# Products that nothing reads in the waits of a chunked scan, and three weight tiles ahead of the fourth in the last stage

## What is computed

```python
def step(state, inp):                      # 8 heads of 64, 1024 positions
    r_t, w_t, k_t, v_t, a_t, b_t = inp
    sa = jnp.einsum('bhvk,bhk->bhv', state, a_t)
    state = state * w_t[:, :, None, :] + sa[..., None] * b_t[:, :, None, :] \
            + v_t[..., None] * k_t[:, :, None, :]
    return state, jnp.einsum('bhvk,bhk->bhv', state, r_t)
...
yn = ((y - mu) * lax.rsqrt(var + GN_EPS)).reshape(B, S, RWKV_WIDTH) * lnx_g + lnx_b
y_a = yn + bonus                           # width 512
br_a = (y_a * jax.nn.silu(z_a)) @ w_pa[l]
br_b = (y_b * jax.nn.silu(z_b)) @ w_pb[l]
merged = jax.nn.sigmoid(g_a) * br_a + jax.nn.sigmoid(g_b) * br_b
x = x + gate[:, None, :] * (merged @ w_o[l])
return rms_norm(x, final_g)
```

## Time and profile before

| | us |
|---|---|
| median of 3 runs | 2534.33 |
| the profiled execution's own time | 2538.74 |
| its span, first to last instruction | 2537.0 |
| TensorE busy | 2445.8 (96%) |
| VectorE / ScalarE / GpSimd busy | 1338.9 / 849.6 / 984.2 |
| mean granted TensorE clock, share of full speed | 0.985 |

### The profile page before, as it was taken

How to read it: one execution, slowest core, us unless ns; L and a number is a source line. 1 busy time by engine, 2 the same in 40 slices (tenths; PEclk the granted TensorE clock), 3 DMA queues, 4 the chain that set the end, 5 groups by cost and what they waited for, 6 DMA issues and landing times. The chain is left out here.

```text
span 2537.0 us, 41052 instructions
## 1 busy us (share of the span) xinstructions
PE 2445.8 (96%) x17413; PEld 1984.2 (78%) x17413; DVE 1338.9 (53%) x2078; ACT 849.6 (33%) x1375; POOL 984.2 (39%) x524
## 2 busy tenths in 40 slices
PE   7998999999999999999999989999999998988998
PEld 6887878888888888888887747787786668887786
DVE  6113543253253221222468289999997764456842
ACT  4214553321111120123453266445333662224231
POOL 3221424443243342344565215466462202221774
PEclk9999999999999999999999999999999998899999
DMA  3112413122222211111323412342343002103423
GB/s 141 49 43 83 134 34 108 50 81 88 78 82 87 75 50 42 50 50 50 103 72 126 133 44 81 104 136 82 106 135 146 26 24 89 37 4 110 149 76 115
DMA packets 82085, 207.68 MB, mean 82 GB/s; under 512 B 8392, under 2 KB 21744, under 8 KB 81904
## 3 DMA queue, kind: packets, MB, share of 16 engines
q1 hardware_dynamic: 74992, 192.48, 23.1%
q10 hardware_dynamic: 6912, 12.59, 1.4%
HBM read 170.81 MB, written 35.27 MB: 81 GB/s over the span
## 5 line engine op out<-in xcount | busy, mean ns | idle before, releaser
L332 PE MATMUL ps<-region_rounded,weights_hi_by_slot 128*128 128x512 f32 x2432 | 962.1, 396 | 19.7 <-DVE region_rounded L640 13.6
L334 PE MATMUL ps<-region_rounded,weights_lo_in_place 128*128 128x512 f32 x2432 | 948.8, 390 | 0.0
L333 PE MATMUL ps<-region_rounded,weights_hi_by_slot 128*128 128x512 f32 x2432 | 948.4, 390 | 0.0
L326 POOL TENSOR_TENSOR weights_lo_in_place<-wbuf,weights_hi_by_slot 128x1024 fp32r<-128x1024 f32 x194 | 483.9, 2497 | 670.0 <-ACT weights_hi_by_slot L322 669.7
L332 PEld LDWEIGHTS ps<-region_rounded,weights_hi_by_slot 128*128 128x128 f32 x2432 | 458.0, 188 | 123.1 <-issue 26.5
L333 PEld LDWEIGHTS ps<-region_rounded,weights_hi_by_slot 128*128 128x128 f32 x2432 | 458.1, 188 | 95.6 <-issue 3.6
L334 PEld LDWEIGHTS ps<-region_rounded,weights_lo_in_place 128*128 128x128 f32 x2432 | 457.6, 188 | 95.9
L322 ACT CAST weights_hi_by_slot<-wbuf 128x1024 fp32r<-128x1024 f32 x194 | 201.8, 1043 | 370.7 <-DMA wbuf<-w_mlp 215.7
L2169 DVE MAX8 gcols<-region 128x8 f32<-128x384 f32 (+5 forms) x192 | 171.6, 894 | 6.6
L2171 DVE MATCH_REPLACE8 region<-gcols,region 128x384 f32<-128x384 f32 (+5 forms) x192 | 168.2, 876 | 0.0
L1459 POOL TENSOR_TENSOR region_rounded<-region,region_rounded 128x512 fp32r<-128x512 f32 x64 | 83.0, 1297 | 215.5 <-DVE region_rounded L1612 215.5
(11 more groups left out here) (368 smaller groups left out, 3459.0 us busy)
## 6 DMA issues: line engine op xcount, KB each, us to landing
wbuf<-w_mlp SPq DMA_DIRECT2D x64, 512.0 KB, 3.6
wbuf<-w_hn SPq DMA_DIRECT2D x37, 512.0 KB, 4.1
wbuf<-w_in SPq DMA_DIRECT2D x25, 512.0 KB, 3.7
region<-xT SPq DMA_DIRECT2D x24, 512.0 KB, 6.4
xtra<-w_ada SPq DMA_DIRECT2D x32, 384.0 KB, 4.2
scratch_hn_out<-tmp ACTq DMA_DIRECT2D x48, 256.0 KB, 3.9
region<-scratch_hn_out SPq DMA_DIRECT2D x24, 512.0 KB, 7.7
wbuf<-w_att SPq DMA_DIRECT2D x20, 512.0 KB, 3.7
```

The costliest lines, as they stand in the source:

```text
L326: self.nc.gpsimd.tensor_tensor(self.m.lo4[:, n % SLOTS, :], self.m.raw4[:, n % SLOTS, :], self.m.hi4[:, n % SLOTS, :].bitcast(F32), ALU.su ...
L332: nc.tensor.matmul(out, m.hi4[:, s, w], m.rounded(hi + k, half(hf)), start=(k == 0), stop=False)
L333: nc.tensor.matmul(out, m.hi4[:, s, w], m.rounded(lo + k, half(hf)), start=False, stop=False)
L334: return nc.tensor.matmul(out, m.lo4[:, s, w], m.rounded(hi + k, half(hf)), start=False, stop=(k == KT - 1))
```

## The change

Two edits, which don't touch each other.

In the second scan `in_use(n)` issues n products of the identity (a 128*128 weight load and 64 columns) into columns 256 to 319 of bank 7, which nothing reads; they wait for no semaphore and set none. Three stand in each level 4 and 5 after the second half's y1 and q1 products and before the wait for the first mask, and three between G and W of each pair. In pair 0 eight stand at each of the four places that hold the state's steps in later pairs. In all 8 x 9 + 32 = 104.

In the last stage the first four groups of branch A (c = 0 and 1, both halves, j = 16 to 19) are issued as tiles 0 to 2 of all four, then tile 3 of all four. The waits for weights and bank stand before tile 0, the count in `st.products` after tile 3. The other groups are as before.

```diff
--- before.py
+++ after.py
@@ -2411,6 +2411,7 @@
 
 
 
+
     S = new_semaphore(nc)
     mats, mats_masked = S("chunk_products"), S("chunk_products_masked")
     turned, tok_copied = S("tok_turned"), S("tok_copied")
@@ -2516,6 +2517,10 @@
 
         @block.tensor
         def _(pe):
+            def in_use(n):
+                for _ in range(n):
+                    nc.tensor.matmul(m.ps[:, 7, 256:320], m.const("ident"), m.const("ident")[:, 0:64], start=True, stop=True)
+
             def chunk_products(i):
                 for par in range(2):
                     if i:
@@ -2597,6 +2602,8 @@
                 if l > 1:
                     before.then_inc(q1, 1)
                 n = 2 * (LAST * i + l - 1)
+                if l > 3:
+                    in_use(3)
                 pe.wait_ge(y1_masked, n + 1)
                 if l == 1:
                     pe.wait_ge(invt_ready, i + 1)
@@ -2689,16 +2697,24 @@
                 chunk_products(i)
                 if i:
                     read_state(2 * i - 2)
+                else:
+                    in_use(8)
                 turn(i)
                 level0(i)
                 if i:
                     use_u(2 * i - 2)
+                else:
+                    in_use(8)
                 level(i, 1)
                 if i:
                     read_state(2 * i - 1)
+                else:
+                    in_use(8)
                 level(i, 2)
                 if i:
                     use_u(2 * i - 1)
+                else:
+                    in_use(8)
                 for l in range(3, LEVELS):
                     level(i, l)
                 apply_inverse(i)
@@ -2919,15 +2935,16 @@
     def rwkv(p, hf):
         return m.chunk(RC + p, half(hf))
 
-    def pair_product(pe, j, n, out_chunk, hf, hi, lo, ready=None):
+    def pair_product(pe, j, n, out_chunk, hf, hi, lo, ready=None, tiles=range(4)):
 
         s, nn = n % SLOTS, out_chunk % 2
-        pe.wait_ge(st.lo_ready, n + 1)
-        if j >= 8:
-            pe.wait_ge(taken, j - 7)
-        else:
-            pe.wait_ge(var, N)
-        for k in range(4):
+        if 0 in tiles:
+            pe.wait_ge(st.lo_ready, n + 1)
+            if j >= 8:
+                pe.wait_ge(taken, j - 7)
+            else:
+                pe.wait_ge(var, N)
+        for k in tiles:
             if ready is not None:
                 ready(k)
             w = slice((nn * 4 + k) * P, (nn * 4 + k + 1) * P)
@@ -2935,7 +2952,8 @@
             nc.tensor.matmul(o, m.hi4[:, s, w], m.rounded(hi + k, half(hf)), start=(k == 0), stop=False)
             nc.tensor.matmul(o, m.hi4[:, s, w], m.rounded(lo + k, half(hf)), start=False, stop=False)
             last = nc.tensor.matmul(o, m.lo4[:, s, w], m.rounded(hi + k, half(hf)), start=False, stop=(k == 3))
-        last.then_inc(st.products, 1)
+        if 3 in tiles:
+            last.then_inc(st.products, 1)
 
     with nc.Block() as block:
         @block.sync
@@ -2974,11 +2992,14 @@
                 for hf in range(2):
                     j = 2 * c + hf
                     pair_product(pe, j, c // 2, c, hf, YB_HI, YB_LO)
-            for c in range(KT):
+            for tiles in (range(3), range(3, 4)):
+                for c in range(2):
+                    for hf in range(2):
+                        pair_product(pe, JA + 2 * c + hf, PASS, c, hf, F_HI, RC,
+                                     (lambda k: pe.wait_ge(y_lo, 2 * k + hf + 1)) if c == 0 else None, tiles)
+            for c in range(2, KT):
                 for hf in range(2):
-                    j = JA + 2 * c + hf
-                    pair_product(pe, j, PASS + c // 2, c, hf, F_HI, RC,
-                                 (lambda k: pe.wait_ge(y_lo, 2 * k + hf + 1)) if c == 0 else None)
+                    pair_product(pe, JA + 2 * c + hf, PASS + c // 2, c, hf, F_HI, RC)
 
             def last_sums(hf):
                 pe.wait_ge(o_added, (KT - 1) * (hf + 1))
```

## The result

Twelve runs of the changed kernel have a median of 2548.45 us (2538.81 to 2553.25), twelve of the kernel before beside them 2534.7 us (2531.78 to 2539.62). The profiled execution took 2549.94 us and spans 2548.1 us at a mean clock of 0.987; that of before spans 2537.0 at 0.985. So 11.1 us more have to be found, and the mean clock is no worse than it was.

A forecast was written before the change was run, and what follows sets the result against it. TensorE was taken as the bound, busy 96% of the span, with lost clock in the second scan and idle time in the last stage. Terms -4.6 + 9.6 - 7.8 = -2.8 us gave 2531.5 us, range 2522.5 to 2538.5.

The forecast's parts named there:

- The price of a fill: Second scan: fills 0.11 us apart, so three push what follows to 0.52 us and eight to 1.07; 9.6 in all.
- The two changes of tile shape: Around fills in a run of 64*64 products: switching to 128*128 and back takes 0.15 us each.
- a change of tiling mode drains TensorE: Rival at the fills: each switch drains the array, 0.28 us more at 28 places, total 2537.5 us; chance 0.10.
- An ordinary pair: Second scan: a pair pays 0.85 us for fills; pairs 1, 2 and 6 regain 4.2 us as the clock holds.
- Pairs 0 and 3: Second scan's pairs with gaps: fills regain 2.9 and 0.7 us of clock loss, against 0.85 each plus 2.8 for eights.
- three quarters, 2.9: Pair 0 of the second scan: fills regain three quarters of the 3.9 us that 1.2 GHz costs there, 2.9 us.
- the quarter for pair 3: Second scan: clock fell at a gap in level 3 without fills, so only a quarter is regained, 0.7 us.
- the 2.8 us for the four eights: Pair 0 of the second scan: four groups of eight fills cost 2.8 us after waits absorb part.
- My rate of 0.23 us for each us at 1.2 GHz: Second scan: each us at 1.2 GHz costs 0.23 us, since much is unscaled waiting; 10.7 us in all.
- the fills do not hold the clock: Rival in the second scan: fills are pure work at 1.2 GHz, 13 us, less 4.6, total 2542.7 us; chance 0.12.
- the fourth rival: Last stage: three tiles first gives nothing, 1 us instead of 4.6, total 2534.5 us; chance 0.10.
- The last stage: Issuing three tiles first saves 4.6 us: 3.1 idle and 1.6 from low clock; bounds 3.3 and 5.06.

The follow-up runs named there:

- s4_one_pass_fills: The changed kernel with each fill's operands viewed as 16-bit (bfloat16) values, same places and counts; 2538.41 us, 1.0014 of the kernel before.
- s1_stage_only: The kernel before with only the last stage's reordering, no fills; 2531.7 us, 0.9984 of the kernel before.
- s3_first_pair_only: The kernel before with only pair 0's four places of eight fills, last stage as before; 2542.38 us, 1.0027 of the kernel before.
- s2_threes_only: The kernel before with only the 24 places of three fills, last stage as before; 2545.46 us, 1.0048 of the kernel before.
- u2: The changed kernel with the second scan's data loads given out pair by pair instead of in two bursts; 2543.99 us, 1.0038 of the kernel before.
- u1_stage_spaced_loads: Reordered last stage without fills, the second scan's data loads given out pair by pair instead of in two bursts; 2536.3 us, 0.9994 of the kernel before.
- v3_threes_spaced: Reordered last stage, scan loads given out pair by pair, plus the 24 places of three fills, no eights; 2535.96 us, 0.9999 of the kernel before.

## Why the prediction was wrong, point by point

**The price of a fill: the term that was mis-read.** I took "7 of them start within 0.92 less the 0.25 us of the last, so 0.11 us apart" for seven products. They were seven records, and each 32-bit product leaves two. The trace of before could have told it: it counts 512 products of L2527 and 16 of L2986, where the code writes 256 (2 x 4 x 2 x 2 = 32 a pair) and 8. The description of the kernel above has the same slip, with 64 products for `chunk_products`. Three fills take 0.96 us instead of 0.52, eight 2.1 instead of 1.07, and all 28 places, at the clock that they had, 38.7 us. The two changes of tile shape were right: 0.15 us in and 0.20 out (2246.84 less the start of the last fill, 2246.03 + 0.88 - 0.275), for a forecast of 0.15 each. The Trainium skill's rule that a change of tiling mode drains TensorE (page "TensorEngine Tiling (Array Packing)", section "Tiling Modes") is not borne out as a full drain here: both distances are below the 0.22 and 0.275 us that the product ahead lasts, and in s4_one_pass_fills two changes and three products fit in 0.34 us. That rival is out.

**An ordinary pair: right, by two errors that cancel.** Pairs 1, 2 and 4 to 7 were to cost 6 x 0.85 - 4.2 = 0.9 us and cost 0.0. These pairs at a clock of 0.99 or 1.00 take 26.0 us on average without fills (9 of them, in before, s1_stage_only and s3_first_pair_only) and 26.5 with three places of three (5 in after; 26.7 for 5 in s2_threes_only): 0.5 to 0.7 us, where 0.85 was forecast from a fill of half the size. The waits take up more of a fill than I had counted. That the clock would hold there was right, with all three places in a pair; with the two in the levels it held in five pairs of six.

**Pairs 0 and 3: the step that failed.** It is "Pair 0 has fills on both sides of its first gap, few around its second: three quarters, 2.9", with the quarter for pair 3, and the 2.8 us for the four eights. Forecast for the two pairs: 0.85 + 2.8 - 2.9 and 0.85 - 0.7, together +0.9 us; measured +17.2. The runs showed in its place: (1) the fills of pair 0 at 2.4 GHz cost 6.6 us (u2 against u1) and not 3.65. (2) The clock fell at the gap all the same, and no fill brought it back. (3) Once it was low, the fills cost 1.8 times as much (3.82 us for 2.08, 1.70 for 0.96), and the low stretch was longer: it lasted 30.7 us from pair 0 on, for 17.0 before and 20.5 in s1_stage_only, with 23.9 in both s2_threes_only and s3_first_pair_only. That the fills are what made it longer is argued from these single profiles, and v3_threes_spaced, with its threes, has 17.0. These two pairs are 16.3 of the 17 us between the forecast and the measured median.

My rate of 0.23 us for each us at 1.2 GHz holds without fills: pair 0 of before against that of u1_stage_spaced_loads is 6.0 us longer, of which 2.64 are its two gaps (1.34 us, and 1.30, not shown), for 17.1 - 3.6 = 13.5 us more at 1.2 GHz (2(1-c)t), so 0.25. With fills it is (12.3 - 1.06)/27.6 = 0.41. The Trainium skill has the penalty as the throttled time by one minus the ratio, so 0.5 for each us (page "TensorE: Matmul & The Clock Gate", section "Terms"); the traces come nearer to that, 0.41, where fills have closed most of TensorE's waits, and stay at half of it where they are open.

The rival that came nearest is the second, "the fills do not hold the clock", 2542.7 us at a chance of 0.12. Its account, 13 us of pure work at 1.2 GHz, is not what happened: they held it in the ordinary pairs, and cost most in two. The price of the fourth rival was added up wrong: 3.6 us less gain on 2531.5 is 2535.1, not 2534.5.

**The last stage: right.** Gain forecast 4.6 us with j = 20 some 11.3 us after j = 16; measured 11.57 and 4.4 in the profile, 4.1 as a kernel of its own. The fourth rival is out.

**What the gaps are, and what stays open.** I had put the gaps that the profile calls "issue" down as unexplained. The DMA rows of the same traces tell more. They show packets of 16,384 bytes of the kind "instruction" on a queue of their own (q8), 54 in the second scan of before. I take them for TensorE's, since there are 138 in the whole program for its 34,826 products and weight loads, one for some 252. The gap in pair 3 of after ends at 2210.27, and the last such packet before it ran from 2207.79 to 2208.87, 6.9 us after the one ahead of it. The DMA view of 2207.7 to 2208.0 us has its start:

```profile
q8 instruction: 1, 0.02, 22.5%
```

There are 28 "issue" gaps of 1.2 us or more in the scans of all 13 profiles, and every one ends 1.2 to 1.5 us after such a packet has landed. By chance that distance would lie anywhere between 0 and the packets' spacing, which is 3.9 us at the median of the scans and 4.4 to 8.0 us ahead of these gaps. So in these gaps TensorE waits for its next instructions. Why the packet is late is less certain: 27 of the 28 have 0.6 to 2.05 MB of data loads in them and in the 3 us ahead, and the packets travel through the same DMA engines, but one gap of 1.37 us (u1_stage_spaced_loads) has none, and spacing the loads moved the gaps and did not end them. A 32-bit fill adds four instructions to this stream (41,468 for 41,052 in the whole program, 104 fills); what that costs was not measured by itself.

The 30.7 us at 1.2 GHz with TensorE busy throughout aren't explained. And where the clock falls differs from one execution to the next: the change's own runs spread over 14 us, and its mean clock goes with them (0.993 at 2538.81 us, 0.987 at 2553.25), so a single profile shows one case of several.

## What to carry to other kernels

Before pricing an instruction from a row, count the row's records against the code: a 32-bit product here is two loads and two products, and what a record costs depends on its type and tile (0.12 us for 128*128 in 32 bits, 0.03 for 128*128 in 16 bits or 64*64 in 32). Where a gap is put down to "issue", look at the instruction packets in the DMA view before anything else. Filler that is to hold a clock must be weighed where the clock is already low, since it costs 1.8 times as much there and didn't restore it here; take the gap away first, or leave the filler out. Moving real work into a wait, as the last stage does, gave its full 4 us with nothing added.

## What was not expected of the hardware

- A 32-bit product of 64 columns behind a 128*128 weight load advances by 0.12 us for each of its two records at 2.4 GHz (0.96 us for three products with two changes of shape) and by (3.67 - 0.42)/15 = 0.22 us at 1.2 GHz.
- TensorE stayed at 1.2 GHz for 30.7 us in which the profile has it busy all the time, eight and then three by three full-array products of the identity among them.
- Gaps of 1 to 3.15 us that the profile puts down to issue, in every profile of this case; all those of 1.2 us or more end 1.2 to 1.5 us after a packet of TensorE's instructions has landed. With the loads spaced out they stand in pairs 1, 2 and 4, in 2, or in 3. Not each one costs the clock: s2_threes_only kept 2.4 GHz through one of 2.21 us in pair 3.
